# Dealing six projection units of the short convolution out between the attention heads of an encoder block

## The chip, the cores and the metric

One core of a Trainium2 chip runs the whole block. The metric is the device time of one execution in microseconds; lower is better. The engines are TensorE (PE: matmuls, and its weight loads as PEld), VectorE (DVE), ScalarE (ACT), GpSimd (POOL) and SyncE (SP), whose queue starts the weight transfers.

## What is computed

One residual block on 512 tokens of 1024 values, all in float32: a SwiGLU feed-forward half step (1024 to 2816 and back), the mixer, a second such half step, and a last RMS norm. Each part begins with an RMS norm whose scale and shift come from a vector c. The mixer, in which the change lies:

```python
z = h @ w_in[l]                                   # 1024 -> 2240 columns
xb, xc, xu, cq, ckv, kr = jnp.split(z, cuts, axis=-1)
y_a = short_conv_mixer(xb, xc, xu, conv_w[l])     # xb * causal 3-tap conv(xc * xu), 512 wide
y_b = mla(cq, ckv, kr, positions, ...)            # 4 heads, keys of 128 + 64 rotary, values of 128
y_a = group_rmsnorm(y_a, g[:512], 8)              # 8 groups of 64
y_b = group_rmsnorm(y_b, g[512:], 4)              # one norm for each head
x = x + g2 * (jnp.concatenate([y_a, y_b], axis=-1) @ w_out[l])
```

In `mla` queries are `rmsnorm(cq) @ w_uq`, keys and values `rmsnorm(ckv) @ w_ukv`; attention is block-causal over chunks of 64 tokens, with a softmax in float32.

## The kernel before, in words

**Units.** Activations lie transposed: 128 features on the partitions, 512 tokens along the row. Weights come in units of up to 128 x 1024 values (512 KB). For each unit SP loads `raw`, ACT copies it rounded into `wh` (`split_hi`, L408), DVE or POOL subtracts to get the rest `wl` (`split_lo`, L1118; POOL's `unit_lo`, L381), and PE multiplies. Each tile of 128 inputs costs three matmuls (high by high, high by low, low by high: `three`, L722), so a unit of eight tiles has 24 matmuls of 512 columns. `raw`, `wh` and `wl` have two buffers each, taken by the parity of the unit's number: the load of unit n waits for the split of n-2 (`lo_ready`), ACT's copy for the product of n-2 (`unit_done`).

**Order.** Every engine has its instructions written out in program order, and runs them in that order; counting semaphores tie them together. Units are numbered: `U_Z` (six units for ckv, cq and the rotary key), `U_CONV` (three for each of the four convolution tiles: C, U, B), `U_V` (two for the values), `U_H` (one for each head: query, query rotary, key), `U_O` (eight half units of the output product), then the second feed-forward. Convolution units run back to back in a loop before `U_V`. For tile i, ACT copies C out of PSUM, DVE multiplies it by U, sums three taps (`cacc`, L1391 and L1394) and multiplies by B into `yc` (L1398).

**Attention.** `head_part(h, 0..2)` makes the query, its rotary part and the key; ACT copies each rounded (`qnh`, `qrh`, `knh`: L570, L574, L576), DVE multiplies the rotary part by cosines (L1434) and subtracts the rests (L1426, L1439, L1441). `scores(h, q)` for four query tiles, longest first; `maximum` on DVE (L1474), `exp` on ACT (L584), `divide` on DVE once the four are done (L1483, L1488), `turn(h, q)` on PE (transposes, L970), `turned_hi` on ACT (L591), `turned_lo` on DVE (L1493), `head_product(h)`. PE interleaves scores(h+1, q) with turn(h, q); parts of heads 2 and 3 stand between.

**Norms.** A norm is a column sum on PE (`norm_sum`, L741) into PSUM bank 7 (`norm_bank`), `root` on ACT (L422), `inverse` on DVE (L1134 to L1146: reciprocal, rounding, rest, two diagonals), `norm_spread` on PE (L748), and `apply` on DVE (L1166), whose result ACT rounds (L432) and DVE subtracts (L1157). The convolution's group norm has `conv_square` (ACT, L536), `conv_sum` (PE, L922, into bank 4), `conv_root` (ACT, L628), `conv_inverse` and `conv_split` (DVE, L1462 to L1469), `conv_spread` (PE, L930 and L931), `apply_conv` (DVE, L1451), `conv_hi` (ACT, L432) and `conv_lo` (POOL, L388). In before the group norm comes first and head 0's norm after it. ACT loads a table when it goes from exponentials to square roots or back (ACT_TABLE_LOAD). `warm` (L755) are nine matmuls with no use but to keep PE at work; one call stands after the value units.

Of the kernel before, what the change touches and what calls it, by code (L numbers as in the profile page):

```python
# [90 lines left out]
FREE = 1  # L91


def hybrid_block(nc, x, c, positions, ada_w, ada_b, norm_ffn1_g, ffn1_w1, ffn1_w3, ffn1_w2, norm_mix_g,
                 w_in, conv_w, q_norm_g, w_uq, kv_norm_g, w_ukv, out_norm_g, w_out, norm_ffn2_g,
                 ffn2_w1, ffn2_w3, ffn2_w2, final_norm_g, consts, out):
    with ExitStack() as ctx:  # L97
# [304 lines left out]
        def _(act):  # L402
# [118 lines left out]
            with act.Fori(0, CT // 2) as m:  # L521
                for s in range(6):
                    p, which = divmod(s, 3)
                    if which == 0:

                        act.wait_ge(unit_done, U_CONV + 6 * m + s + 1)
                        act.wait_ge(u_conv, FREE + 2 * m + p)
                        act.activation(cbuf[:, :], pb[CONV_BANKS[p][0]][:, :], ACT.Copy).then_inc(c_copied, 1)
                    split_hi(U_CONV + 6 * m + s + 2, s % 2, 48 * m + landed(U_CONV + s + 2))
# [1101 lines left out]
```

## Time and profile before

| | us |
|---|---|
| median of 3 runs | 1052.82 |
| lowest, highest | 1052.28, 1054.54 |
| span of the profiled execution | 1052.8 |
| PE busy | 1009.5 (96%) |
| PE weight loads busy | 831.4 (79%) |
| DVE busy | 564.9 (54%) |
| ACT busy | 400.6 (38%) |
| POOL busy | 66.3 (6%) |
| mean granted clock of PE | 0.974 |

The profile gives no time of the profiled execution other than its span, which is the median of the runs to 0.02 us; nothing lies around it to be added. Busy shares are of the whole span, so they say which engine is near its limit, but a stage has to be looked at by itself: by stretches of time (with the clock granted to PE, 1.00 for 2.4 GHz and 0.50 for 1.2), by the waits of PE, and by the instructions in order of time. In such rows "[1.23 <-DVE ubuf]" means that the engine was idle for 1.23 us just before, until that instruction of DVE was done. A matmul of 512 columns is shown with 0.39 us but the next starts 0.23 behind it.

### The profile page before, as it was taken

The page shows a single profiled execution, that of the slowest core. Times are in us where ns is not written, and L with a number is a line of the kernel's source. Part 1 is how long each engine was busy: PE and PEld are TensorE (multiplying, and loading weights), DVE is VectorE, ACT ScalarE, POOL GpSimd, SP SyncE. Part 2 cuts the span into 40 slices and gives each one's busy share as a digit, 9 for nine tenths or more (in the row PEclk, how much of TensorE's full clock was granted, in tenths as well). Part 3 has the DMA queues.
Part 4 walks back from the last instruction along what each step waited for, and adds up shares of the span by engine and source line. Part 5 has one row for each costly group of instructions (what it writes and reads, how often), then busy time and mean ns, then how long its engine had stood idle before and what let it go on. Part 6 is the DMA issues. An engine that isn't in the chain of part 4 may idle for free. (4 is left out here: it accounts for less than half of the span.)

```text
span 1052.8 us, 13254 instructions
## 1 busy us (share of the span) xinstructions
PE 1009.5 (96%) x4505; PEld 831.4 (79%) x4505; DVE 564.9 (54%) x754; ACT 400.6 (38%) x568; POOL 66.3 (6%) x79
## 2 busy tenths in 40 slices
PE   3699999999999999999999989999999999999997
PEld 3678888888888888888867777788888888888886
DVE  5868777787753333754377645744434333333332
ACT  3254434444332222442255443353444444332222
POOL 2411111011000000000000310000000000000000
PEclk9599999999999999999999799999999999999999
DMA  9547766687633324123221101223323333333232
GB/s 333 175 133 249 242 198 211 206 256 235 202 92 93 92 90 115 50 81 100 80 65 40 41 23 58 80 80 100 98 85 96 99 100 100 94 93 93 90 109 81
DMA packets 176622, 127.82 MB, mean 121 GB/s; under 512 B 5069, under 2 KB 165718, under 8 KB 176598
## 3 DMA queue, kind: packets, MB, share of 16 engines
q1 hardware_dynamic: 168534, 98.14, 31.1%
q0 software_dynamic: 8064, 29.36, 8.4%
q8 instruction: 14, 0.23, 0.1%
q14 instruction: 10, 0.08, 0.0%
HBM read 125.39 MB, written 2.10 MB: 121 GB/s over the span
## 5 line engine op out<-in xcount | busy, mean ns | idle before, releaser
L722 PE MATMUL pb<-hh,wh 128*128 128x512 f32 x912 | 358.5, 393 | 5.0 <-DVE hl L1159 2.8
L722 PE MATMUL pb<-hh,wl 128*128 128x512 f32 x912 | 355.8, 390 | 0.0
L722 PE MATMUL pb<-hl,wh 128*128 128x512 f32 x912 | 355.7, 390 | 0.0
L1118 DVE TENSOR_TENSOR wl<-raw,wh 128x1024 fp32r<-128x1024 f32 x156 | 191.1, 1225 | 275.1 <-ACT wh L408 275.0
L408 ACT ACTIVATE wh<-raw 128x1024 fp32r<-128x1024 f32 x163 | 172.5, 1059 | 410.5 <-PE pb L722 410.5
L722 PEld LDWEIGHTS pb<-hh,wh 128*128 128x128 f32 x912 | 171.5, 188 | 46.5 <-DVE hl L1159 7.2
L722 PEld LDWEIGHTS pb<-hh,wl 128*128 128x128 f32 x912 | 171.6, 188 | 36.2
L722 PEld LDWEIGHTS pb<-hl,wh 128*128 128x128 f32 x912 | 171.7, 188 | 34.5
L722 PE MATMUL pb<-gh,wh 128*128 128x512 f32 x352 | 137.0, 389 | 0.0
L722 PE MATMUL pb<-gh,wl 128*128 128x512 f32 x352 | 136.9, 389 | 0.0
L722 PE MATMUL pb<-gl,wh 128*128 128x512 f32 x352 | 136.9, 389 | 0.0
L722 PEld LDWEIGHTS pb<-gl,wh 128*128 128x128 f32 x352 | 66.1, 188 | 13.8
L722 PEld LDWEIGHTS pb<-gh,wl 128*128 128x128 f32 x352 | 66.1, 188 | 13.7
L722 PEld LDWEIGHTS pb<-gh,wh 128*128 128x128 f32 x352 | 66.1, 188 | 13.7
L1193 DVE SCALAR_TENSOR_TENSOR acc<-ada_ring,silu_c,acc 128x1024 f32<-128x1024 f32 x49 | 62.8, 1282 | 1.0
L1237 DVE TENSOR_TENSOR gbuf<-sbuf,pb 128x512 f32<-128x512 f32 x44 | 30.2, 686 | 58.4 <-PE pb L722 58.3
L445 ACT ACT_TABLE_LOAD x44 | 56.5, 1283 | 0.8
L417 ACT ACTIVATE sq<-xres 128x512 f32<-128x512 f32 (+1 forms) x32 | 20.2, 631 | 90.2 <-DVE xres L1247 85.2
L373 POOL DMA_DIRECT2D ada_ring<-in_ada_w_dram x56 | 29.8, 532 | 211.3 <-DVE acc L1191 112.8
L1247 DVE SCALAR_TENSOR_TENSOR xres<-pb,half_gates,xres 128x512 f32 (+1 forms) x16 | 12.0, 751 | 46.3 <-PE pb L722 46.3
L452 ACT ACTIVATE gh<-gbuf 128x512 f32 x44 | 27.9, 634 | 10.7 <-DVE gbuf L1237 10.7
L1240 DVE TENSOR_TENSOR gl<-gbuf,gh 128x512 f32 (+1 forms) x44 | 30.1, 683 | 0.0
(193 smaller groups left out, 763.2 us busy)
## 6 DMA issues: line engine op xcount, KB each, us to landing
raw<-in_ffn_w_dram SPq DMA_DIRECT2D x104, 512.0 KB, 3.8
ada_ring<-in_ada_w_dram POOLq DMA_DIRECT2D x56, 512.0 KB, 5.1
raw<-in_ffn_w_dram SPq DMA_DIRECT2D x32, 448.0 KB, 3.4
raw<-in_w_in_dram SPq DMA_DIRECT2D x17, 512.0 KB, 3.9
ada_start<-in_ada_w_dram SPq DMA_DIRECT2D x8, 1024.0 KB, 16.4
raw<-in_w_out_dram SPq DMA_DIRECT2D x8, 512.0 KB, 3.4
x_nat<-in_x_dram SPq DMA_DIRECT2D x1, 2048.0 KB, 10.5
out_dram<-o_nat SPq DMA_DIRECT2D x8, 256.0 KB, 2.9
```

The lines of the kernel that those rows point to most:

```text
L373: pool.dma_start(ada_ring[:, k % 4, :], adav[:, k, bass.ds(j * D_MODEL + 2 * D_MODEL, D_MODEL)]) \
L408: act.activation(wh[par][:, :], raw[par][:, :], ACT.Copy).then_inc(hi_ready, 1)
L417: act.activation(sq[:, slot, :], src, ACT.Square).then_inc(sq_ready, 1)
L445: act.activation(vcol[:, V_COLS + 9:V_COLS + 10], kst[:, K_COLS:K_COLS + 1], ACT.Sigmoid)
L452: act.activation(gh[:, bass.ds(i, 1), :], gbuf[:, :].unsqueeze(1), ACT.Copy).then_inc(gh_ready, 1)
L722: last = pe.matmul(o, a, b, start=start and j == 0 and t == 0, stop=stop and j == len(pairs) - 1 and t == 2)
L1118: dve.tensor_tensor(wl[par][:, :], raw[par][:, :], wh[par][:, :].bitcast(F32), ALU.subtract).then_inc(lo_ready, 1)
L1193: dve.scalar_tensor_tensor(out=acc[:, :], in0=src, scalar=silu_c[:, k:k + 1], in1=acc[:, :], op0=ALU.mult, op1=ALU.add).then_inc(ada_step, 1)
L1237: dve.tensor_tensor(gbuf[:, :], sbuf[:, :], pb[1][:, :], ALU.mult).then_inc(g_ready, 1)
L1240: dve.tensor_tensor(gl[:, bass.ds(i, 1), :], gbuf[:, :].unsqueeze(1), gh[:, bass.ds(i, 1), :].bitcast(F32), ALU.subtract).then_inc(gl_read ...
L1247: dve.scalar_tensor_tensor(out=xd, in0=pb[bank][:, :].unsqueeze(1), scalar=gate, in1=xd, op0=ALU.mult, op1=ALU.add).then_inc(x_upd, 1)
```

## The change

The six units of convolution tiles 2 and 3 (c20 to c22, c30 to c32) leave the loop ahead of the value units and stand between the steps of the heads: c20 before head 0's parts, c21 before head 1's, quarters of c22 behind the score steps of head 0, quarters of c30 behind those of head 1, quarters of c31 behind the transposes of head 0, c32 after head 0's product. Parts of heads 2 and 3 move behind c32. All four orders and SP's loads are rewritten to match; `head_parts_hi`, `head_parts_lo` and the helpers that interleaved scores and transposes become single steps. The key now goes through bank 0. Head 0's norm comes before the group norm, whose column sums now go to `norm_bank` (so `conv_sum(0)` waits for the instruction that applies head 0's norm), and its spreads stand before and inside the first output unit. The nine warm matmuls after the value units are gone. In the diff below the two long orders of ACT and DVE are given as they are after the change, without the lines removed.

```diff
-U_V = U_CONV + 3 * CT
-U_H = U_V + KT
-U_O = U_H + HEADS
+U_V = U_CONV + 3 * (CT // 2)
+LATE = ("c20", "h0", "c21", "h1", "c22", "c30", "c31", "c32", "h2", "h3")
+U_LATE = {name: U_V + KT + j for j, name in enumerate(LATE)}
+U_H = tuple(U_LATE[f"h{h}"] for h in range(HEADS))
+U_O = U_V + KT + len(LATE)
 U_A2 = U_O + DT
...
-AP_BASE = {N_FFN1: 0, N_MIX: 8, N_KV: 16, N_Q: 18, N_HEAD: 25, N_FFN2: 29, N_FINAL: 37}
-AP_CONV = 21
-SPREAD = {N_FFN1: 0, N_MIX: 1, N_KV: 2, N_Q: 3, N_HEAD: 8, N_HEAD + 1: 9, N_HEAD + 2: 10, N_HEAD + 3: 11, N_FFN2: 12}
-SPREAD_CONV = 4
+AP_BASE = {N_FFN1: 0, N_MIX: 8, N_KV: 16, N_Q: 18, N_HEAD: 21, N_HEAD + 1: 26, N_HEAD + 2: 27, N_HEAD + 3: 28,
+   N_FFN2: 29, N_FINAL: 37}
+AP_CONV = 22
+AP_OUT = tuple(AP_CONV + j for j in range(CT)) + tuple(AP_BASE[N_HEAD + h] for h in range(HEADS))
+SPREAD = {N_FFN1: 0, N_MIX: 1, N_KV: 2, N_Q: 3, N_HEAD: 4, N_HEAD + 1: 9, N_HEAD + 2: 10, N_HEAD + 3: 11, N_FFN2: 12}
+SPREAD_CONV = 5
...
-CONV_BANKS = ((0, 1, 2), (3, 4, 6))
+CONV_BANKS = ((0, 1, 2), (3, 4, 6), (6, 2, 6), (2, 1, 2))
...
+    conv_load(U_LATE["c20"], 2, 0)
+    head_load(0)
+    conv_load(U_LATE["c21"], 2, 1)
+    head_load(1)
+    conv_load(U_LATE["c22"], 2, 2)
+    conv_load(U_LATE["c30"], 3, 0)
+    conv_load(U_LATE["c31"], 3, 1)
+    conv_load(U_LATE["c32"], 3, 2)
+    head_load(2)
+    head_load(3)
...
+    unit_lo(U_O)
     conv_lo(0)
-    unit_lo(U_O)
+    unit_lo(U_O + 1)
     conv_lo(1)
     conv_lo(2)
-    unit_lo(U_O + 1)
     conv_lo(3)
...
+    def conv_copy(i):
+        act.wait_ge(unit_done, U_LATE[f"c{i}0"] + 1)
+        if i == 2:
+            act.wait_ge(u_ready, AP_BASE[N_Q] + QT)
+        else:
+            act.wait_ge(conv_step, FREE + 3 * i)
+        act.activation(cbuf_late[:, :], pb[CONV_BANKS[i][0]][:, :], ACT.Copy).then_inc(c_copied, 1)
...
+    for t in range(QT):
+        norm_hi(AP_BASE[N_Q] + t, cqh[:, t, :])
+    act.wait_ge(kr_dup, 1)
+    act.activation(krh[:, :], pb[5][:, :], ACT.Copy).then_inc(krh_ready, 1)
+    unit_hi(U_LATE["c20"])
     for t in range(TT):
         act.wait_ge(unit_done, U_V + KT)
         act.activation(vh[:, t, :], pb[t][:, :], ACT.Copy).then_inc(vh_ready, 1)
+    head_hi(0)
+    conv_copy(2)
+    unit_hi(U_LATE["c21"])
+    nope_hi(0)
+    rope_hi(0)
+    key_hi(0)
     head_hi(1)
+    unit_hi(U_LATE["c22"])
+    nope_hi(1)
+    rope_hi(1)
+    key_hi(1)
+    unit_hi(U_LATE["c30"])
+    for q in range(TT):
+        exp(0, q)
+    unit_hi(U_LATE["c31"])
+    for q in range(TT):
+        exp(1, q)
+    conv_copy(3)
+    turned_hi(0, 0)
+    unit_hi(U_LATE["c32"])
+    turned_hi(0, 1)
+    turned_hi(0, 2)
+    turned_hi(0, 3)
+    conv_square(0)
+    conv_square(1)
     head_hi(2)
     head_out(0)
     head_square(0)
+    head_hi(3)
+    nope_hi(2)
+    rope_hi(2)
+    root(N_HEAD, V_HEAD)
+    key_hi(2)
+    unit_hi(U_O)
+    head_norm_hi(0)
+    exp(2, 0)
+    turned_hi(1, 0)
+    nope_hi(3)
+    exp(2, 1)
+    conv_square(2)
+    turned_hi(1, 1)
+    rope_hi(3)
+    exp(2, 2)
+    conv_square(3)
+    turned_hi(1, 2)
+    key_hi(3)
+    exp(2, 3)
+    turned_hi(1, 3)
+    conv_root()
     unit_hi(U_O + 1)
     head_out(1)
+    head_square(1)
+    for q in range(TT):
+        turned_hi(2, q)
+        exp(3, q)
+    conv_hi(0)
+    conv_hi(1)
+    head_out(2)
+    conv_hi(2)
     conv_hi(3)
     unit_hi(U_O + 2)
+    turned_hi(3, 0)
+    turned_hi(3, 1)
     root(N_HEAD + 1, V_HEAD)
...
+            three(pb[0][:, :], [(cols(wh[b], k), cols(wl[b], k), cqh[:, k, :], cql[:, k, :])
+                                for k in range(QT)], True, True).then_inc(q_done, 1)
         elif part == 1:
-            pe.wait_ge(q_roped, h)
+            if h == 0:
+                pe.wait_ge(vl_ready, 2)
+            else:
+                pe.wait_ge(q_roped, h)
+            if h == 2:
+                pe.wait_ge(u_conv, FREE + CT)
...
-            pe.wait_ge(pl_ready, 3 * (h - 1) + part + 1)
-        if part < 2:
-            three(pb[part][:, :], [(cols(wh[b], QT * part + k), cols(wl[b], QT * part + k), cqh[:, k, :], cql[:, k, :])
-                                   for k in range(QT)], True, True).then_inc(q_done, 1)
-        else:
-            three(pb[2][:, :], [(cols(wh[b], 2 * QT + k), cols(wl[b], 2 * QT + k), ckh[:, k, :], ckl[:, k, :])
+            pe.wait_ge(pl_ready, 3 * h + 1)
+            three(pb[0][:, :], [(cols(wh[b], 2 * QT + k), cols(wl[b], 2 * QT + k), ckh[:, k, :], ckl[:, k, :])
...
+    def late_bank_free(i, which):
+        if i == 2 and which == 1:
+            pe.wait_ge(vl_ready, 3)
+        if (i, which) in ((2, 2), (3, 2)):
+            pe.wait_ge(c_copied, i + 1)
+        if i == 3 and which == 0:
+            pe.wait_ge(u_conv, FREE + 3)
+        if i == 3 and which == 1:
+            pe.wait_ge(q_roped, 2)
+    def conv_quarter(i, which, quarter):
+        n = U_LATE[f"c{i}{which}"]
+        b = n % 2
+        if quarter == 0:
+            unit(n)
+            late_bank_free(i, which)
+        ks = range(2 * quarter, 2 * quarter + 2)
+        last = three(pb[CONV_BANKS[i][which]][:, :], [(cols(wh[b], k), cols(wl[b], k), hh[:, k, :], hl[:, k, :]) for k in ks],
+                     quarter == 0, quarter == 3)
+        if quarter == 3:
+            last.then_inc(unit_done, 1)
+    def conv_unit(i, which):
+        for quarter in range(4):
+            conv_quarter(i, which, quarter)
...
     def conv_sum(j):
         pe.wait_ge(csq_ready, j + 1)
         if j == 0:
-            pe.wait_ge(u_conv, FREE + CT)
-        pe.matmul(pb[4][SQUARE * j:SQUARE * (j + 1), :], kst[:, K_HALF:K_HALF + SQUARE], sq[:, j % 2, :],
+            pe.wait_ge(u_ready, AP_BASE[N_HEAD] + 1)
+        pe.matmul(norm_bank[SQUARE * j:SQUARE * (j + 1), :], kst[:, K_HALF:K_HALF + SQUARE], sq[:, j % 2, :],
                   start=True, stop=True).then_inc(group_summed, 1)
...
+        if h == 0 and q == 1:
+            pe.wait_ge(yc_ready, FREE + 3)
...
-    conv_sum(0)
-    conv_sum(1)
     v_unit(0)
     v_unit(1)
-    warm(WARM_HEADS)
-    head_part(0, 0)
+    conv_unit(2, 0)
+    head_unit(0)
+    conv_unit(2, 1)
+    head_unit(1)
+    for q in range(TT):
+        scores(0, q)
+        conv_quarter(2, 2, q)
+    for q in range(TT):
+        scores(1, q)
+        conv_quarter(3, 0, q)
+    for q in range(TT):
+        turn(0, q)
+        conv_quarter(3, 1, q)
+    head_product(0)
+    conv_unit(3, 2)
+    head_part(2, 0)
+    head_sum(0)
+    head_part(2, 1)
+    norm_spread(N_HEAD)
+    head_part(2, 2)
+    conv_sum(0)
+    scores(2, 0)
+    turn(1, 0)
+    head_part(3, 0)
+    conv_sum(1)
+    scores(2, 1)
+    turn(1, 1)
+    head_part(3, 1)
     conv_sum(2)
-    head_part(0, 1)
+    scores(2, 2)
+    turn(1, 2)
+    head_part(3, 2)
     conv_sum(3)
-    head_part(0, 2)
-    head_unit(1)
-    scores(0, 0)
-    for q in range(1, TT):
-        scores(0, q)
-        head_part(2, q - 1)
-    scores_and_turns(0)
-    head_product(0)
-    head_unit(3)
-    scores_and_turns(1, {0: lambda: conv_spread(0), 2: lambda: conv_spread(1), 3: lambda: conv_spread(2)})
+    scores(2, 3)
+    turn(1, 3)
     head_product(1)
+    for q in range(TT):
+        scores(3, q)
+        turn(2, q)
+    conv_spread(0)
+    head_product(2)
+    conv_spread(1)
+    out_begin(0)
+    out_steps(0, (0,))
+    conv_spread(2)
+    out_steps(0, (1,))
     conv_spread(3)
-    head_sum(0)
-    scores_and_turns(2)
-    norm_spread(N_HEAD)
-    head_product(2)
-    out_unit(0)
-    head_sum(1)
+    out_steps(0, (2, 3)).then_inc(unit_done, 1)
     turn(3, 0)
     turn(3, 1)
+    head_sum(1)
     out_begin(1)
     out_steps(1, (0, 1))
     turn(3, 2)
     turn(3, 3)
+    norm_spread(N_HEAD + 1)
     out_steps(1, (2, 3)).then_inc(unit_done, 1)
     head_product(3)
-    norm_spread(N_HEAD + 1)
     out_begin(2)
+    head_sum(2)
     out_steps(2, (0, 1))
-    head_sum(2)
+    norm_spread(N_HEAD + 2)
     out_steps(2, (2, 3)).then_inc(unit_done, 1)
-    norm_spread(N_HEAD + 2)
...
+    dve.wait_ge(krh_ready, 1)
+    dve.tensor_tensor(krl[:, :], pb[5][:, :], krh[:, :].bitcast(F32), ALU.subtract).then_inc(krl_ready, 1)
+    unit_lo(U_LATE["c20"])
     for t in range(TT):
         dve.wait_ge(vh_ready, t + 1)
         dve.tensor_tensor(vl[:, t, :], pb[t][:, :], vh[:, t, :].bitcast(F32), ALU.subtract).then_inc(vl_ready, 1)
+    head_lo(0)
+    unit_lo(U_LATE["c21"])
+    nope_lo(0)
+    turn_rope(0)
+    rope_lo(0)
+    key_lo(0)
     head_lo(1)
+    conv_u(2, U_LATE["c21"], cbuf_late, cbuf_late)
+    unit_lo(U_LATE["c22"])
+    nope_lo(1)
+    conv_taps(2, cbuf_late, yc[:, 2, :])
+    turn_rope(1)
+    rope_lo(1)
+    key_lo(1)
+    unit_lo(U_LATE["c30"])
+    for q in range(TT):
+        maximum(0, q)
+    conv_y(2, U_LATE["c22"], yc[:, 2, :])
+    maximum(1, 0)
+    unit_lo(U_LATE["c31"])
+    maximum(1, 1)
+    divide(0)
+    maximum(1, 2)
+    maximum(1, 3)
+    turned_lo(0, 0)
+    unit_lo(U_LATE["c32"])
+    turned_lo(0, 1)
+    turned_lo(0, 2)
+    turned_lo(0, 3)
+    conv_u(3, U_LATE["c31"], cbuf_late, cbuf_late)
+    conv_taps(3, cbuf_late, yc[:, 3, :])
+    divide(1)
+    head_lo(2)
+    conv_y(3, U_LATE["c32"], yc[:, 3, :])
+    head_lo(3)
+    nope_lo(2)
+    turn_rope(2)
+    rope_lo(2)
+    inverse(N_HEAD)
+    key_lo(2)
+    apply_head(0)
+    maximum(2, 0)
+    turned_lo(1, 0)
+    nope_lo(3)
+    maximum(2, 1)
+    turned_lo(1, 1)
+    turn_rope(3)
+    rope_lo(3)
+    maximum(2, 2)
+    turned_lo(1, 2)
+    key_lo(3)
+    maximum(2, 3)
+    turned_lo(1, 3)
+    divide(2)
     conv_inverse(0)
+    maximum(3, 0)
+    conv_inverse(1)
+    turned_lo(2, 0)
+    maximum(3, 1)
     conv_inverse(2)
+    turned_lo(2, 1)
+    maximum(3, 2)
     conv_inverse(3)
+    turned_lo(2, 2)
+    maximum(3, 3)
     conv_split()
+    turned_lo(2, 3)
+    apply_conv(0)
+    divide(3)
+    apply_conv(1)
+    apply_conv(2)
     apply_conv(3)
+    turned_lo(3, 0)
+    turned_lo(3, 1)
     inverse(N_HEAD + 1)
+    turned_lo(3, 2)
+    turned_lo(3, 3)
     apply_head(1)
     inverse(N_HEAD + 2)
     apply_head(2)
```

## Rows read from the trace of the kernel before

**Rows 1.** The page, busy time of each engine.

```profile
PE 1009.5 (96%) x4505; PEld 831.4 (79%) x4505; DVE 564.9 (54%) x754; ACT 400.6 (38%) x568; POOL 66.3 (6%) x79
```

**Rows 2.** Windows of the core: length, busy times, PEclk, DMA share, GB/s.

```profile
531.30:618.30 87.00, 83.38 (x362) 63.10 (x361) 59.58 (x130) 46.11 (x106) 9.83 (x6) 0.90 0.13 40
...
573.80:577.20 3.40, 3.40 (x13) 3.16 (x14) 2.26 (x4) 2.05 (x4) 0.00 (x0) 0.56 0.00 0
591.30:604.90 13.60, 12.35 (x37) 9.40 (x38) 8.94 (x16) 6.13 (x12) 7.21 (x5) 0.50 0.23 78
632.20:635.60 3.40, 3.40 (x11) 2.75 (x10) 0.69 (x1) 0.99 (x2) 0.00 (x0) 0.50 0.24 83
```

**Rows 3.** Waits of PE from 498 to 670 us: total, times, longest.

```profile
PE pb L748 <- DVE diag L1146: 2.4, 2, 2.3
PE pb L741 <- DVE ubuf L1451: 1.2, 1, 1.2
PE pb L722 <- DVE wl L1118: 1.2, 1, 1.2
PE pb L722 <- DVE ptl L1493: 1.1, 2, 0.8
PE pb L722 <- ACT probs L584: 0.8, 1, 0.8
PE pb L922 <- ACT sq L536: 0.4, 1, 0.4
```

**Rows 4.** PE in order of time: the first conv sums, the warm matmuls.

```profile
533.10 1.56 PE L922 MATMUL pb<-sq,kst 128*32 128x512 f32 x4 [0.36 <-ACT sq L536]
...
540.21 1.75 PE L755 MATMUL pb<-exact 128*128 128x384 f32 x9
```

**Rows 5.** ACT in order of time: start, length, instruction, idle before.

```profile
515.15 1.06 ACT L408 ACTIVATE wh<-raw 128x1024 fp32r<-128x1024 f32 x1 [4.38 <-PE pb L722]
...
531.47 1.06 ACT L408 ACTIVATE wh<-raw 128x1024 fp32r<-128x1024 f32 x1 [4.38 <-PE pb L722]
...
536.53 0.63 ACT L432 ACTIVATE cqh<-ubuf 128x512 fp32r<-128x512 f32 x1 [0.76 <-DVE ubuf L1166]
...
599.09 1.28 ACT L422 ACT_TABLE_LOAD   x1
600.39 0.26 ACT L422 ACTIVATE rms<-pb,kst 128x4 f32<-128x4 f32 x1
...
606.50 0.69 ACT L584 ACTIVATE probs<-pb,nmax_s 128x512 f32<-128x512 f32 x1
```

**Rows 6.** DVE in order of time.

```profile
532.56 1.23 DVE L1118 TENSOR_TENSOR wl<-raw,wh 128x1024 fp32r<-128x1024 f32 x1 [0.23 <-ACT wh L408]
...
550.66 0.69 DVE L1441 TENSOR_TENSOR knl<-pb,knh 128x512 fp32r<-128x512 f32 x1 [0.29 <-ACT knh L576]
...
578.84 0.94 DVE L1462 RECIPROCAL sq<-sq 128x128 f32<-128x128 f32 x1
...
593.25 4.44 DVE L1488 TENSOR_SCALAR probs<-probs,rinv 128x512 f32<-128x512 f32 x4
...
600.68 0.18 DVE L1134 RECIPROCAL rrms<-rms 128x4 f32<-128x4 f32 x1 [2.33 <-ACT rms L422]
...
601.79 0.68 DVE L1146 TENSOR_TENSOR diag<-kst,rrms_l 128x512 fp32r<-128x512 f32 x1
...
611.06 1.27 DVE L1488 TENSOR_SCALAR probs<-probs,rinv 128x512 f32<-128x512 f32 x4
...
631.29 0.75 DVE L1166 SCALAR_TENSOR_TENSOR ubuf<-o_raw,vcol,pb 128x512 f32<-128x512 f32 x1 [0.64 <-issue]
```

**Rows 7.** The page, transfers of w_in: KB each, us to landing.

```profile
raw<-in_w_in_dram SPq DMA_DIRECT2D x17, 512.0 KB, 3.9
```

**Rows 8.** POOL in order of time.

```profile
593.87 1.38 POOL L388 TENSOR_TENSOR hl<-ubuf,hh 128x512 fp32r<-128x512 f32 x1 [0.37 <-ACT hh L432]
595.21 2.40 POOL L381 TENSOR_TENSOR wl<-raw,wh 128x1024 fp32r<-128x1024 f32 x1
```

More of the change, by code:

```diff
@@ L189, in hybrid_block @@
         assert e3 <= 229344, e3
+        (cbuf_late,), _ = place(region + 2 * KT * SEQ * 4, ("cbuf_late", [P, SEQ], F32))
         (xg,), _ = place(hh_at, ("xg", [P, DT, SEQ], F32))
@@ L519, in _, with unit_hi @@
             root(N_Q, Q_LORA)
[L521 to L529, printed above, removed]
+            for s in range(6):
+                i, which = divmod(s, 3)
+                if which == 0:
+                    act.wait_ge(unit_done, U_CONV + s + 1)
+                    act.wait_ge(u_conv, FREE + i)
+                    act.activation(cbuf[:, :], pb[CONV_BANKS[i][0]][:, :], ACT.Copy).then_inc(c_copied, 1)
+                split_hi(U_CONV + s + 2, s % 2, landed(U_CONV + s + 2))
+            def unit_hi(n):
+                split_hi(n, n % 2, landed(n))
+            def conv_copy(i):
[5 more added lines that the diff above has]
+                act.activation(cbuf_late[:, :], pb[CONV_BANKS[i][0]][:, :], ACT.Copy).then_inc(c_copied, 1)
             def conv_square(j):
@@ L548, in head_hi @@
             def head_hi(h):
-                b = h % 2
-                n = U_H + h
+                n = U_H[h]
+                b = n % 2
+                before = sum(U_H[g] % 2 == b for g in range(h))
                 act.wait_ge(raw_landed[b], landed(n))
-                act.wait_ge(kn_landed[b], 16 * (h // 2 + 1))
+                act.wait_ge(kn_landed[b], 16 * (before + 1))
                 act.wait_ge(unit_done, n - 1)
@@ L593, in turned_hi @@
                                ACT.Copy).then_inc(pth_ready, 1)
-            def exps_and_turned(h, behind=None):
-                for q in range(TT):
-                    turned_hi(h, q)
-                    exp(h + 1, q)
-                    if behind is not None and q in behind:
-                        behind[q]()
             def head_out(h):
@@ L981, in head_product @@
                 last.then_inc(pv_done, 1)
-            def scores_and_turns(h, behind=None):
-                for q in range(TT):
-                    scores(h + 1, q)
-                    turn(h, q)
-                    if behind is not None and q in behind:
-                        behind[q]()
             def head_sum(h):
                 pe.wait_ge(gsq_ready, h + 1)
-                norm_sum(N_HEAD + h, gsq, AP_BASE[N_HEAD] + h)
+                norm_sum(N_HEAD + h, gsq, AP_BASE[N_HEAD + h])
             def out_begin(o):
@@ new lines, in conv_y @@
+            def conv_y(i, n, sums):
+                dve.wait_ge(conv_step, FREE + 3 * i + 3)
+                dve.wait_ge(unit_done, n + 1)
+                dve.tensor_tensor(yc[:, i, :], sums[:, :], pb[CONV_BANKS[i][2]][:, :], ALU.mult).then_inc(yc_ready, 1)
+            for s in range(6):
+                i, which = divmod(s, 3)
+                if which == 1:
+                    conv_u(i, U_CONV + s, cbuf, ubufc)
+                if which == 2:
+                    conv_taps(i, ubufc, cacc)
+                    conv_y(i, U_CONV + s, cacc)
+                split_lo(U_CONV + s + 2, s % 2)
@@ L1532, in _ @@
-            maxima_and_turned(1, {0: lambda: apply_conv(0), 2: lambda: apply_conv(1), 3: lambda: apply_conv(2)}, first=1)
-            divide(2)
-            apply_conv(3)
-            inverse(N_HEAD)
-            maxima_and_turned(2)
-            divide(3)
-            apply_head(0)
-            for q in range(TT):
-                turned_lo(3, q)
+            turned_lo(2, 3)
[3 more added lines that the diff above has]
+            apply_conv(2)
+            apply_conv(3)
```

195 lines of the change are left out of this document (68 added, 127 removed).

## The prediction

> **What bounds the kernel now.** I read the page's busy times first: TensorE (PE) is busy 96% of the span [rows 1], so a new order of the same matmuls can only pay by filling PE's idle time or by getting back a slow clock. Next the granted clock by stretch: in the 87 us between the last convolution unit and the end of the first output unit PE runs at 1.2 GHz instead of 2.4 for 3.4 us and again for 13.6 us, and once more for 3.4 us behind that [rows 2]. Then the PE waits from the projection to the end of the output product: 7.1 us in six groups [rows 3]. Last the order of ScalarE (ACT), VectorE (DVE) and GpSimd (POOL) in that stretch, because the diff rewrites all four queues. The profiled execution spans 1052.8 us, the median of the runs is 1052.82, so sum and median are taken against the same time. 0.2% (2.1 us) is about what a measurement of this kernel can tell from no change.
>
> **What PE executes.** The same matmuls in another order, less the nine warm matmuls, which last 1.7 us [rows 4]. One unit of 24 matmuls takes 5.44 us (three units lie between the ACT splits at 515.15 and 531.47 [rows 5]), a quarter unit 1.36. So the sum is: waits and slow clock taken away, against waits and slow clock made. I follow the new queues in the time of before, up to the end of the first output unit (618.3), where both orders have done the same work.
>
> **Gone, at most.** Warm 1.7. The waits of before up to 618.3: 7.1 less the 2.4 and the 1.2 behind it, 3.5 [rows 3]. The slow clock: (3.4 + 13.6 − 1.2 idle) / 2 = 7.9 [rows 2, 3]. Together 13.1.
>
> **Made, one by one.** PE runs in program order, so each wait below holds everything behind it.
> 1. The first late unit (c20). The value units now end at 538.3: they lose the two conv sums ahead of them, which began at 533.1 behind a wait of 0.4 and took 1.5 [rows 4], and start 1.9 earlier. ACT writes the last query tile until 537.16, then krh (0.5 more), then the unit's split (1.06); DVE's half takes 1.23 [rows 5, 6]: ready at 540.0. Wait 1.7, just what the warm matmuls filled.
> 2. Heads 0 and 1: each step of scores or transposes has a dense quarter behind it. DVE's new work there (six splits of 1.23, the product, the taps) fits: 0.3 us for scores(0,2), whose exponential stands behind the split of c30; otherwise nothing, and ACT and DVE have one to three us of slack at each step. The SP queue issues the same loads, only reordered; each waits for the split two units before, some 5 us before its turn, and lands in 3.9 [rows 5, 7]. Cost 0. If that cover is gone, a late load costs at most its 3.9 once.
> 3. **norm_spread of head 0.** This is the large one. It stands between parts 1 and 2 of head 2, and needs root(N_HEAD), which on ACT stands behind rope_hi(2), which needs the DVE product on part 1. So from the issue of part 1's last matmul: 0.2 until it is drained, 0.69 product, 0.63 copy, 1.28 table load (square root after exponentials), 0.26 root, 1.79 inverse and diagonals (600.68 to 602.47) [rows 5, 6] = 4.85; the spread's first half can issue before the second diagonal is there, which gives 0.15 back. Wait 4.7.
> 4. **conv_sum(0)** now writes norm_bank, so it waits for apply_head(0), which on DVE stands behind key_lo(2), that is behind part 2, the matmuls just ahead: 0.2 + 0.6 + 0.69 + 0.75 = 2.25 [rows 5, 6].
> 5. conv_sum(3): its square stands on ACT behind exp(2,2), which hangs by a chain of nine short steps (about 5.0 us, copies and subtractions of 0.4 to 0.7) against 3.8 of PE work: 1.15. Then head_product(1), behind exp(2,3) and the last transpose's two copies: 1.7.
> 6. scores(3,2) behind the table load and exp(3,0): 1.28 + 0.69 + 0.2 after the transposes' copy [rows 5], against one step of PE work: 1.2 (0.8 in before [rows 3]).
> 7. conv_spread(0): four reciprocals of 0.94 and the split (about 1.1) now lie among the maxima of head 3 instead of in idle time: they end 2.15 after the last transpose [rows 6].
> 8. The first output unit. Before, its inputs were ready long ahead. Now apply_conv, ACT's copy and POOL's subtraction (1.3 to 1.4) run just ahead of the matmuls, and divide(3) stands between apply_conv(0) and (1) while POOL makes a unit split of 2.4. The row of before for just that pair is 4.44 us for the four scalings where 1.27 is normal, ending with POOL's instruction (597.69 and 597.61) [rows 6, 8]. I take 4.4: waits of 0.4, 2.0, 1.35 and 1.6 = 5.35. With 1.27 it would be 2.2.
>
> Sum of new waits: 1.7 + 0.3 + 4.7 + 2.25 + 2.85 + 1.2 + 2.15 + 5.35 = 20.5.
>
> One rule speaks to points 3 and 6. Rows: the table load takes 1.28 and the root begins 0.02 behind it [rows 5]. The Trainium skill, ScalarE: Activation LUTs, What ACT_TABLE_LOAD costs, adds a drain of about 1.38 us to each switch. By that page point 3 would be about 6.1, an estimate; the rows show no such gap, and the sum stays with 1.28.
>
> **The clock, made.** Before, a wait of 2.4 with short matmuls around it was followed by 3.4 us at half clock, and one of 0.8 amid scores and transposes likewise [rows 2, 3]. A fall costs (3.4)/2 = 1.7. I expect one fall after points 3 and 4, one after 5 and 6, one in 7 and 8: 5.1. Bounds: none, 0; or half clock throughout from point 5 on, as in the 13.6 us of before, when PE's about 22 us of work there cost up to 10 more, less what the waits absorb.
>
> **Behind the first output unit.** norm_spread(N_HEAD+1) now stands earlier, and ACT's root ahead of the last transposes; POOL's split no longer falls on the diagonals (the 2.4 of before). Its wait becomes 1.1, the next spread's 0.6: −0.7; the 3.4 us of slow clock behind it go: −1.7. Together −2.4. The 1.2 behind DVE's split of an output unit stays. From there on nothing differs.
>
> **Sum.** −13.1 + 20.5 + 5.1 − 2.4 = +10.1: 1052.8 + 10.0, rounded = **1062.8 us**. The heads 0 and 1 do what interleaving should do, but head 0's norm chain in series costs more than it wins.
>
> **Rivals.**
> A. *Density wins* (faster). The dense quarters keep the clock at 2.4 GHz all through, and ACT and DVE run far enough ahead that only points 1, 3 and 4 are left: −13.1 − 2.4 + 1.7 + 7.0 = −6.8: 1046. For it: the 17 us of slow clock lie where scores and transposes stand alone [rows 2]. Against: head 3's scores and head 2's transposes still stand alone, and points 7 and 8 are chains through three engines. It decides if all waits but those of points 1, 3 and 4, and the clock's cost, stay below 6.8 us together. The Trainium skill, TensorE: Matmul & The Clock Gate, says that the default clock is the throttled one and activity releases it, which favours this rival; the trace agrees only in part: in the 13.6 us at half clock PE was busy for 12.35 [rows 2]. Chance 0.12.
> B. *Waits real, clock full, the chain at the output unit short* (divide(3) gets through before POOL locks it out). −13.1 + 20.5 − 3.15 − 1.0 − 2.4 = +0.85, where the 3.15 are point 8's 5.35 less 2.2, and the 1.0 is absorbed in points 5 to 7: 1053.7. Chance 0.10, half of it within 0.2%.
> C. *The clock stays down* from point 3 to the output unit: +10 where the forecast has +5.1, and a fall of 1.7 in the tail: 1069. For it: 12 us of waits in the last 20 us before that point. Chance 0.13.
> The forecast (one to three falls, and a few us either way in the waits, 1056 to 1067): 0.65.
>
> **Range.** From between B and the forecast's foot to C: 1053 to 1071; outside it A and a little above C, under 0.2. Faster 0.13 (A and a bit of B), same 0.06, slower 0.81.
>
> **What the profile would show.** Right: PE's wait for the diagonals of head 0 near 4.7 us between parts 1 and 2 of head 2, 2.2 for conv_sum(0), waits for POOL's hl in the first output unit, no wait over 0.5 in heads 0 and 1, full clock there, two more table loads. Wrong: PE waits in that stretch below 13 us together, or slow clock over 15 us from head 2 on, or DVE or ACT late already in head 1 (splits of the late units as the wait), which would make it slower in a place I hold free.

## The result, and the profile after

The changed kernel takes 1063.91 us (median of 4, 1062.52 to 1064.40) against 1053.09 (median of 4, 1052.28 to 1054.54): ratio 1.0103, 95% interval 1.0090 to 1.0116. It is slower by 10.8 us. The profiled execution spans 1062.1 us, and its own time is 1063.8: 1.7 us lie around the span, as in every later run that gives both. So the span of before, 1052.8, belongs to an execution of about 1054.5, one of its longest, and not to the median as the prediction had it. Comparing the two profiles gives 9.3 us of loss instead of 10.8. The same kernel's executions differ by 3 to 4 us, which has to be kept in mind for every difference below 2 us. In some of the variants below the longer executions have the lower mean clock; in the kernel before the two do not go together (about 1051.3 at 0.976, 1052.8 at 0.980, 1054.5 at 0.977).

The page of the changed kernel, busy times:

```profile
PE 1009.0 (95%) x4496; PEld 827.0 (78%) x4496; DVE 565.4 (53%) x754; ACT 403.9 (38%) x570; POOL 66.4 (6%) x79
```

PE is busy as long as before [rows 1] in a longer span, without its nine warm matmuls. ACT has two instructions more, the two table loads. The waits of PE from 498 to 670 us (total, times, longest):

```profile
PE pb L807 <- DVE diag L1255: 4.2, 1, 4.2
PE pb L781 <- DVE wl L1227: 3.0, 2, 1.8
PE pb L1014 <- DVE ubuf L1275: 2.2, 1, 2.2
PE pb L1022 <- DVE group_rl L1584: 1.8, 1, 1.8
PE pb L781 <- DVE ptl L1608: 1.4, 1, 1.4
PE pb L781 <- POOL hl L410: 1.3, 1, 1.3
PE pb L781 <- ACT probs L620: 1.0, 1, 1.0
PE pb L1014 <- ACT sq L570: 0.2, 1, 0.2
PE pb L781 <- POOL wl L403: 0.2, 1, 0.2
```

This answers to [rows 3]. The two large ones at the diagonals and at `ubuf` are head 0's norm; `wl` holds the first late unit (1.8) and the unit of 1.2 that was there before; the rest stand one each at head_product(1), scores(3,2), conv_spread(0), the first output unit and conv_sum(3). Windows of the changed kernel: from the new first late unit to c32's end, the heads 2 and 3 up to conv_spread(0), then up to the end of the first output unit, the tail, and three stretches at half clock:

```profile
498.60:565.50 66.90, 65.08 (x300) 52.51 (x300) 41.16 (x81) 30.15 (x63) 0.00 (x0) 1.00 0.25 68
565.50:612.40 46.90, 36.10 (x156) 24.64 (x154) 25.92 (x56) 23.43 (x48) 2.36 (x1) 0.93 0.10 34
612.40:630.70 18.30, 17.03 (x45) 11.16 (x46) 7.49 (x10) 3.01 (x5) 7.52 (x5) 0.63 0.10 30
630.70:648.50 17.80, 17.46 (x91) 14.30 (x90) 8.99 (x17) 7.51 (x13) 4.78 (x2) 1.00 0.18 59
574.60:578.00 3.40, 3.07 (x7) 2.27 (x8) 0.88 (x2) 0.00 (x0) 0.00 (x0) 0.54 0.00 0
581.50:584.90 3.40, 3.40 (x8) 2.09 (x7) 1.72 (x1) 1.13 (x1) 1.17 (x1) 0.52 0.32 91
612.60:626.30 13.70, 13.70 (x33) 8.73 (x33) 6.64 (x8) 2.38 (x4) 6.25 (x4) 0.51 0.13 39
```

In heads 0 and 1 the clock is 1.00 and PE is idle only once. Then come 46.9 us with 36.1 of work. The first output unit ends at 630.7 instead of 618.3 (12.4 later), and in the tail about 3.1 us come back: the 2.4 at the diagonals is a wait no more, nor is there a stretch at half clock [rows 2, 3].

Head 0's norm chain in the changed kernel, ACT and DVE in order of time (start, length):

```profile
571.45 0.63 ACT L608 ACTIVATE qrh<-rope 128x512 fp32r<-128x512 f32 x1 [3.06 <-DVE rope L1547]
572.10 1.28 ACT L444 ACT_TABLE_LOAD   x1
573.39 0.27 ACT L444 ACTIVATE rms<-pb,kst 128x4 f32<-128x4 f32 x1
```

```profile
570.72 0.69 DVE L1547 TENSOR_TENSOR rope<-pb,cs 128x512 f32<-128x512 f32 x1 [1.38 <-PE pb L781]
...
573.69 0.18 DVE L1243 RECIPROCAL rrms<-rms 128x4 f32<-128x4 f32 x1 [0.89 <-ACT rms L444]
...
579.32 0.69 DVE L1556 TENSOR_TENSOR knl<-pb,knh 128x512 fp32r<-128x512 f32 x1 [3.85 <-ACT knh L612]
579.93 0.74 DVE L1275 SCALAR_TENSOR_TENSOR ubuf<-o_raw,vcol,pb 128x512 f32<-128x512 f32 x1
```

Rotary product, copy, table load, root, inverse, each begins when the one before it ends. conv_sum(0) then starts at 580.81, right behind the last row.

### The profile page after: what moved, and what is told of

It is laid out like the page before. It is cut to its first block, busy times and chain, and to the rows that moved or that the text cites. A ratio compares the mean times of both kernels' runs of the same rounds, so it can differ in the third digit from the quotient of the medians.

```text
span 1062.1 us, 13114 instructions
## 1 busy us (share of the span) xinstructions
PE 1009.0 (95%) x4496; PEld 827.0 (78%) x4496; DVE 565.4 (53%) x754; ACT 403.9 (38%) x570; POOL 66.4 (6%) x79
## 4 chain that ended last, share of the span: by engine, by line
PE 86%; DVE 3%; ACT 2%; issue 2%; POOL 0%; POOLq 0%; DVEq 0%; ACTq 0%
PE pb L781 83%; DVE ubuf L1275 1%; PE pb L814 1%; DVE hl L1268 1%; ACT wh L430 0%; PE pb L800 0%; PE pb L807 0%; PE pb L1041 0%; PE pb L1014 0%; DVE wl L1227 0%; POOL hl L410 0%; ACT L444 0%; POOLq L103 0%; PE pb L1207 0%; POOL wl L403 0%
## 5 line engine op out<-in xcount | busy, mean ns | idle before, releaser
L781 PEld LDWEIGHTS pb<-gh,wh 128*128 128x128 f32 x352 | 66.1, 188 | 13.9
L781 PEld LDWEIGHTS pb<-gh,wl 128*128 128x128 f32 x352 | 66.1, 188 | 13.7
L781 PEld LDWEIGHTS pb<-gl,wh 128*128 128x128 f32 x352 | 66.1, 188 | 13.6
L403 POOL TENSOR_TENSOR wl<-raw,wh 128x1024 fp32r<-128x1024 f32 x5 | 11.9, 2384 | 312.6 <-ACT wh L430 312.6
```

What stands on the lines that cost most here:

```text
L403: pool.tensor_tensor(wl[n % 2][:, :], raw[n % 2][:, :], wh[n % 2][:, :].bitcast(F32), ALU.subtract).then_inc(lo_ready, 1)
L781: last = pe.matmul(o, a, b, start=start and j == 0 and t == 0, stop=stop and j == len(pairs) - 1 and t == 2)
```

## The experiments

Twelve kernels ran, all of them told here, each against the kernel before. "Changed" is the changed kernel. Times are medians, in us.

**1. The norm chain out of series (e1_chain).** On the changed kernel:

```diff
 # PE
-head_part(2, 1); norm_spread(N_HEAD); head_part(2, 2); conv_sum(0); scores(2, 0); turn(1, 0)
+head_part(2, 1); head_part(2, 2); norm_spread(N_HEAD); turn(1, 0); scores(2, 0); conv_sum(0)
 # ACT
-nope_hi(2); rope_hi(2); root(N_HEAD, V_HEAD); key_hi(2)
+nope_hi(2); root(N_HEAD, V_HEAD); rope_hi(2); key_hi(2)
 # DVE
-nope_lo(2); turn_rope(2); rope_lo(2); inverse(N_HEAD); key_lo(2)
+nope_lo(2); inverse(N_HEAD); turn_rope(2); rope_lo(2); key_lo(2)
```

> Head 0's norm chain taken out of series: ACT's root(N_HEAD) stands before rope_hi(2), DVE's inverse before the rotary product of head 2, and PE makes part 2 of head 2, then norm_spread, turn(1, 0) and scores(2, 0) before conv_sum(0). Theory (the waits of 4.2 and 2.2 us for this chain, and the two falls of the clock behind them, are a large part of the loss): the two waits shrink to about 2 together and one fall at least goes, 1063.9 - 4.4 - 1.7 to 3.4 = 1056 to 1058. Rival (the work behind is held by ACT and DVE anyway, so PE only arrives earlier at later waits): 1062 to 1064, with the 6.4 us found again in the waits at conv_sum(3), head_product(1) and conv_spread(0).

Measured 1054.37 (10 runs, 1052.57 at a mean clock of 0.981 to 1057.82 at 0.971), ratio to before 1.0014 (1.0002 to 1.0027). Waits of PE, the largest:

```profile
PE pb L781 <- DVE wl L1227: 3.0, 2, 1.8
PE pb L781 <- DVE knl L1556: 1.5, 1, 1.5
PE pb L781 <- DVE ptl L1608: 1.4, 1, 1.4
```

The 6.4 us have become 1.5, at scores(2,0), and 9.5 us are won, more than the waits and two falls of the clock. The rival, that the time would be found again further on, falls.

**2. The old order of the norms, the units still dealt out (v2_oldnorm).** The group norm first, head 0's norm behind it:

```diff
-AP_BASE: N_HEAD: 21; AP_CONV = 22; SPREAD: N_HEAD: 4; SPREAD_CONV = 5
+AP_BASE: N_HEAD: 25; AP_CONV = 21; SPREAD: N_HEAD: 8; SPREAD_CONV = 4
 # PE
-head_part(2, 0); head_sum(0); head_part(2, 1); norm_spread(N_HEAD); head_part(2, 2)
+head_unit(2)
...
 out_steps(0, (2, 3)).then_inc(unit_done, 1)
+head_sum(0)
...
 out_steps(1, (0, 1))
+norm_spread(N_HEAD)
 # ACT and DVE: root, inverse and apply of the heads moved back to match
```

> The dealing out of the six units kept, the order of the norms as in the kernel before: group norm first, head 0's norm behind it (its sum after the first output unit, its spread inside the second, the other heads' norms moved back to match). Theory (of the two parts of the change the order of the norms is the one that costs): the waits of 4.2 and 2.2 us and the falls behind them go, and about 1 to 2 us of new waits come in the tail: 1063.9 - 6.4 - 3.4 + 2 = 1056. Rival (the dealing out itself costs, by the squeezed group norm between the heads and the output unit): 1060 or more.

Measured 1055.09 (10 runs, 1052.15 to 1056.75), ratio 1.0022 (1.0010 to 1.0034). So of the 10.8 us the way the norms stand costs 8.8, and the dealing out, as it is done here, 2.0 to 2.4 (in this series the kernel before took 1052.68). It is not the order as such: e1_chain keeps head 0's norm first and takes no longer. The remaining waits of v2_oldnorm include 1.8 at the group's rest, 1.4 at head_product(1) and 1.8 at the first late unit, as in the changed kernel.

**3. What the clock costs (w1_fill, w2_fill, w3_fill).** Warm matmuls put into the waits; no order moves:

```diff
 head_part(2, 1)
+warm(22)                    # w1, w3
 norm_spread(N_HEAD)
 head_part(2, 2)
+warm(11)                    # w1, w3
 conv_sum(0)
...
+warm(7, 2)                  # w3, ahead of head_product(1)
...
+warm(5, 2)                  # w2, w3, ahead of scores(3, 2)
...
+warm(9, 2)                  # w2, w3
 conv_spread(0)
```

> Warm matmuls put into two waits of the changed kernel: 22 before norm_spread of head 0 (wait 4.2 us) and 11 before conv_sum(0) (wait 2.2 us). No order is changed and no wait gets shorter, so this measures the clock alone. Theory (idle time behind these waits brings the clock down for two stretches of 3.4 us): both falls go, 2 to 3.4 us faster, 1060.5 to 1062. Rival (the clock falls for another reason, as the short matmuls of the scores): 1064.

> Warm matmuls put into the wait for exp(3, 0) (5) and the wait before conv_spread(0) (9) of the changed kernel. Theory (the 13.6 us at half clock from conv_spread(0) on follow from idle time before it): the stretch goes or is one of 3.4 us, and since the units behind then wait for POOL and DVE a little more, 3 to 6 us faster: 1058 to 1061. Rival (it follows from scores and transposes, which keep PE busy with short matmuls, as before the change): 1064, with the same stretch at 0.50.

> The changed kernel with all its larger waits between head 2 and the output unit filled with warm matmuls: 22 before norm_spread of head 0, 11 before conv_sum(0), 7 before head_product(1), 5 before scores(3, 2), 9 before conv_spread(0). No order changes. Theory (the clock is a third of the loss): the granted clock is 1.00 all through and 4 to 6 us are won against the changed kernel, 1058 to 1060. Rival (only the falls behind head 0's norm cost, those further on are covered by the chain through DVE, ACT and POOL): 1060 to 1061, as with two fills.

w1_fill: 1060.66 (1059.82 to 1061.36), 3.3 below the changed kernel. In its profile both falls behind head 0's norm are gone, and conv_sum(3) starts 26.7 instead of 29.4 us behind head_sum(0): they were worth 2.7. What else it won came later, where it has 3.4 and 6.8 us at half clock instead of 13.7. w3_fill: 1060.07 (1059.76 to 1061.57), 3.8 below; in its profiled execution, one of the long ones (1061.52), 3.4 us at half clock lie at 508 and 6.8 in the first output unit, so the clock was not full all through as expected.

w2_fill: 1063.97, but its four executions are two at 1061.5 and 1062.5 with a mean clock of 0.981 and 0.978, and two at 1065.5 and 1065.7 with 0.972, so the median tells nothing. Its profile (1062.47) does: no half clock from conv_spread(0) to the first output unit's end, and that stage lasts 15.4 us where the changed kernel has 18.3. The stage and PE's waits in it:

```profile
613.90:629.30 15.40, 11.14 (x44) 7.36 (x45) 7.54 (x10) 3.01 (x5) 7.53 (x5) 1.00 0.10 36
PE pb L781 <- POOL hl L410: 2.7, 3, 1.3
PE pb L1022 <- DVE ubuf L1569: 1.5, 1, 1.5
```

So the 13.7 us at half clock cost 2.9 there, not the 6.8 that half their length would be: PE's idle time in the stage is 4.3 without them and 1.3 with them. One execution of each shows this.

**4. The lock (x_div, w4_fill_div).** In both divide(3) goes behind the four apply_conv; w4_fill_div has the fills of w3_fill besides.

```diff
 apply_conv(0)
-divide(3)
 apply_conv(1)
 apply_conv(2)
 apply_conv(3)
+divide(3)
```

> The changed kernel with one step moved on DVE: divide(3) behind apply_conv(3) instead of between apply_conv(0) and apply_conv(1). In the changed kernel these four scalings last 4.4 us (1.3 alone), ending with POOL's unit split, while apply_conv(1) waits behind them. Theory (the first output unit is bound by the chain spread, apply, round, subtract, of which this lock is the longest link, and not by the slow clock, since filling the waits ahead took the slow clock away and won nothing): apply_conv(1) comes 3 to 4 us earlier and 1.5 to 3 us are won: 1061 to 1062.5. Rival (the slow clock sets that stage): 1064, since PE's work at half clock covers the chain.

> As w3_fill, and divide(3) behind apply_conv(3). With the clock kept up, the price of the lock stands alone. Theory (the chain at the first output unit counts once the clock does not cover it): apply_conv(1) comes some 4 us earlier, the waits there fall from about 4.5 to about 2.5, and 2 us are won against w3_fill. Rival (the next links, POOL's subtraction behind each spread, are as late): same as w3_fill.

x_div: 1064.28 (1062.36 to 1066.24), no gain in the median. w4_fill_div: 1058.32 (1056.54 to 1058.55) against w3_fill's 1059.76 to 1061.57: 1.8 us, as the theory said, and the ranges do not touch. DVE in w3_fill, and then in w4_fill_div:

```profile
612.85 4.42 DVE L1609 TENSOR_SCALAR probs<-probs,rinv 128x512 f32<-128x512 f32 x4
617.19 0.73 DVE L1572 SCALAR_TENSOR_TENSOR ubuf<-yc,vcol,pb 128x512 f32<-128x512 f32 x1
```

```profile
613.34 0.75 DVE L1572 SCALAR_TENSOR_TENSOR ubuf<-yc,vcol,pb 128x512 f32<-128x512 f32 x1 [1.98 <-PE pb L1023]
```

Counted from conv_spread(0) (611.2 and 609.8), the second apply_conv comes at 6.0 and at 3.5. The stage up to the first output unit's end takes 17.2 and 13.9 us:

```profile
611.20:628.40 17.20, 14.19 (x45) 9.13 (x46) 7.56 (x10) 3.01 (x5) 7.54 (x5) 0.80 0.09 31
```

```profile
609.80:623.70 13.90, 11.12 (x44) 7.37 (x45) 5.55 (x10) 3.01 (x5) 7.45 (x5) 1.00 0.12 39
```

Part of this difference is clock (0.80 against 1.00), which is why the medians differ by less. The same stage in five profiles:

| | divide(3) | us at half clock | PE idle | length |
|---|---|---|---|---|
| changed | ahead | 13.7 | 1.3 | 18.3 |
| w3_fill | ahead | 6.8 | 3.0 | 17.2 |
| w2_fill | ahead | none | 4.3 | 15.4 |
| x_div | behind | 3.4 | 1.9 | 14.5 |
| w4_fill_div | behind | none | 2.8 | 13.9 |

At full clock divide(3) in its old place costs 1.5 us (15.4 against 13.9), the slow clock alone 2.9 (18.3 against 15.4). The theory of x_div holds in this stage. It does not show in the median: x_div's profiled execution has 10.2 us at half clock behind head 0's norm where the changed kernel has 6.8, and 3.4 more on the way, and comes to conv_spread(0) at 614.6 instead of 612.4.

**5. The first late unit (x_c20).** ACT's and DVE's halves of c20's split moved ahead of the last query tile's copy and of krh and krl:

```diff
-for t in range(QT): norm_hi(...); krh; unit_hi(c20)   # ACT
+for t in range(QT): norm_hi(...), behind t == 1: unit_hi(c20); krh
-krl; unit_lo(c20)                                     # DVE
+unit_lo(c20); krl
```

> The changed kernel with the split of the first late unit ahead of the last query tile's copy and of the rotary key on ACT, and ahead of the rotary key's rest on DVE. Theory (PE's wait of 1.8 us for this unit is ACT's and DVE's order): the wait falls to about 0.8 to 1.0 and 0.8 to 1.0 us are won, 1063. Rival (the value units or the transfer hold it): no change of the wait.

The wait falls from 1.8 to 1.0, as expected; DVE still has the query tiles' rests ahead of the split. 1062.68 (1060.80 to 1063.19), 1.2 below the changed kernel, of which 0.8 is the wait; the rest is within the scatter.

**6. The warm matmuls (b_nowarm).** The kernel before without `warm(WARM_HEADS)`.

> The kernel before without its nine warm matmuls behind the value units. Theory of the prediction's sum (the 1.7 us of warm matmuls are PE time that can be had back only where nothing else is awaited): part 0 of head 0 waits for its split, ready 0.5 us behind the value units, so 1.1 us are won, 1051.9. Rival (the wait behind the warm matmuls brings the clock down or the vl subtractions hold the parts): 1053 or more.

1052.74 (1051.35 to 1054.80), ratio 0.9999 (0.9990 to 1.0008): nothing. The theory falls. Behind the value units PE now waits for the value rests:

```profile
541.83 0.47 PE L722 MATMUL pb<-cqh,wh 128*128 128x512 f32 x1 [1.50 <-DVE vl L1511]
```

The part starts at 541.83; in before, behind the warm matmuls, at 541.88. From there on both kernels have the same orders, so their profiles also show what half clock is worth. The 3.4 us at half clock from 573.8 on are missing here, and everything behind comes 1.6 us earlier. The 13.6 us of before are 6.8 here, and that brings only 0.2 more, for PE's wait at head 0's column sum is 3.4 instead of 1.2:

```profile
PE pb L741 <- DVE ubuf L1450: 3.4, 1, 3.4
```

**7. A version that beats both (c1_early, c2_early, c3_early).** From v2_oldnorm with x_c20's edit; the group norm pulled forward:

```diff
 # PE, c1
-head_unit(2); conv_sum(0); scores(2, 0); turn(1, 0); head_part(3, 0); conv_sum(1); scores(2, 1) ...
+head_part(2, 0); conv_sum(0); head_part(2, 1); conv_sum(1); head_part(2, 2); turn(1, 0); conv_sum(2)
+scores(2, 0); conv_sum(3); head_part(3, 0); scores(2, 1) ...
-for q: scores(3, q); turn(2, q)
+for q: scores(3, q); turn(2, q); conv_spread(q)
 # PE, c1: the first output unit runs without spreads between its steps
 # ACT, c1: conv_square(2), (3) and conv_root() to ahead of exp(2, 0); conv_hi among the steps of head 3
 # DVE: conv_inverse(0..3) among the steps of head 2, conv_split() ahead of maximum(3, 0), divide(3) behind apply_conv(3)
 # PE, c2
-head_product(1); scores(3, 0)
+scores(3, 0); head_product(1)
 # PE, c2: norm_spread(N_HEAD) from behind out_steps(1, (0, 1)) to behind turn(3, 3)
 # ACT, c2: turned_hi(1, 1) behind rope_hi(3); exp(3, 0) ahead of unit_hi(U_O + 1)
 # DVE, c2
-maximum(2, 1); conv_inverse(2); turned_lo(1, 1); turn_rope(3); rope_lo(3); maximum(2, 2); conv_inverse(3)
+maximum(2, 1); turn_rope(3); rope_lo(3); turned_lo(1, 1); maximum(2, 2); conv_inverse(2)
 # PE, c3
-for q: ...; turn(2, q); conv_spread(q); then head_product(2)
+for q: ...; turn(2, q); conv_spread(q - 1); then head_product(2); conv_spread(3)
 # DVE, c3
-inverse(N_HEAD); turned_lo(3, 0); turned_lo(3, 1)
+turned_lo(3, 0); turned_lo(3, 1); inverse(N_HEAD)
 # DVE, c3: apply_conv(0..2) one score step later
 # ACT, c3
-root(N_HEAD); head_square(1); turned_hi(3, 0); turned_hi(3, 1)
+turned_hi(3, 0); turned_hi(3, 1); root(N_HEAD); head_square(1)
```

> The dealing out kept, the norms in the order of before, and the group norm pulled forward: its sums stand between the parts of head 2, its root ahead of exp(2, 0), its reciprocals among the steps of head 2 and its spreads behind the four score steps of head 3, so that the first output unit finds its inputs ready; the first late unit's split ahead of the rotary key; divide(3) behind the spreads. Theory (what the dealing out wins by a full clock in heads 0 and 1 was eaten by the norms that it pushed together): waits at the group's rest (1.8) and in the first output unit (1.2) and 0.8 at the first late unit go against v2_oldnorm, 1055.1 - 3 to 4 = 1051 to 1052, below the kernel before by 1 to 2 us. Rival (the two more table loads and the denser DVE queue in head 2 make new waits of the same size): 1054 to 1056.

> c1_early with its one large wait (3.9 us at head_product(1)) attacked: head 3's rotary product goes ahead of the transposes' copies on DVE and ACT, two of the group's reciprocals move behind, and scores(3, 0) stands ahead of head_product(1). Theory (that wait is the DVE order): it falls below 1, one fall of the clock goes with it, 1050.5 - 3 to 4 = 1047. Rival (DVE is simply full there, 3.9 us of reciprocals more than before): 1049.5 to 1051, the wait found again before conv_spread(0).

> c2_early with its two new waits attacked: each group spread stands one score step later and the last behind head_product(2), so that the group's rest (wait of 1.9 us) is ready; and head 0's inverse goes behind the first two transposes' rests on DVE, so that these, which read PSUM, no longer stand behind scalings that POOL's unit split holds up (wait of 2.2 us at turn(3, 2)). Theory: both waits fall below 0.5 and the time to 1047, 0.5% below the kernel before. Rival (the waits only move, to the first output unit, whose last input now comes later, and to the spread of head 0): 1049 to 1050.

c1_early: 1050.47, ratio 0.9972 (0.9961 to 0.9982). The waits at the group's rest and in the first output unit are gone, a new one of 3.9 stands at head_product(1). c2_early: 1049.69, with 12 executions from 1046.30 to 1054.96, ratio 0.9974 (0.9959 to 0.9989); its 3.9 is gone, but 1.4 now stands at scores(3, 0), and 1.9 and 2.2 at the group's rest and at turn(3, 2). Against c1_early this is no gain that can be told, as the rival said. c3_early: **1045.40** (5 runs, 1045.02 to 1046.27), ratio 0.9929 (0.9915 to 0.9942). Its waits of PE above 0.3 us:

```profile
PE pb L782 <- DVE wl L1229: 2.2, 2, 1.2
PE pb L782 <- DVE knl L1558: 1.4, 1, 1.4
PE pb L808 <- DVE diag L1257: 1.0, 1, 1.0
PE pb L782 <- DVE hl L1270: 0.9, 3, 0.4
```

The 1.9 and the 2.2 are gone. The 2.2 was for the most part a matter of order and not of POOL: in c2_early DVE stood idle until head 0's root was there (613.65), which on ACT came ahead of the transposes' copies, then made the inverse, and only then the rests that PE waited for. POOL held up one step in this by 0.5 us. c3_early is 7.5 us faster than the kernel before and 18.5 faster than the changed one, so with the norms rearranged the units can be dealt out at a gain. No run has the rearranged norms without the dealing out, so how much of the 7.5 each brings is not shown.

## Why the prediction was right

1062.8 was forecast with a range of 1053 to 1071, and 1063.91 was measured. Of the signs named, those of being right came: the waits for head 0's diagonals and for conv_sum(0), a wait for POOL's `hl`, no wait over 0.5 and full clock in heads 0 and 1, two more table loads. But one sign of being wrong came too: 20.5 us at half clock from head 2 on, where over 15 was to count against it, and the waits (13.9) are just above the 13 that was to do so. By its time this is the forecast's case, by its clock rival C's. The sum was right to 1 us (+10.1 against +10.8 by the medians and +9.3 by the two profiles), but its terms were not: two errors of 5 to 7 us cancelled. That was partly luck and partly one and the same effect, as the clock took the place of waits.

- **Waits.** Forecast 20.5, measured 13.9 up to the first output unit's end (the table above without the 1.2 and the 0.2 behind it). Point by point: the first late unit 1.7 and 1.8; heads 0 and 1 0.3 and none; norm_spread of head 0 4.7 and 4.2; conv_sum(0) 2.25 and 2.2; conv_sum(3) 1.15 and 0.2; head_product(1) 1.7 and 1.4; scores(3,2) 1.2 and 1.0; conv_spread(0) 2.15 and 1.8. All eight are within 1 us. The term that was mis-sized is **point 8**, 5.35 against 1.3. Its mechanism is there: divide(3) takes 4.40 us in the changed kernel, ending with POOL, as in the row of before [rows 6, 8]:

```profile
614.47 4.40 DVE L1603 TENSOR_SCALAR probs<-probs,rinv 128x512 f32<-128x512 f32 x4
618.79 0.73 DVE L1566 SCALAR_TENSOR_TENSOR ubuf<-yc,vcol,pb 128x512 f32<-128x512 f32 x1
```

```profile
615.09 1.33 POOL L410 TENSOR_TENSOR hl<-ubuf,hh 128x512 fp32r<-128x512 f32 x1 [32.42 <-ACT hh L454]
616.39 2.40 POOL L403 TENSOR_TENSOR wl<-raw,wh 128x1024 fp32r<-128x1024 f32 x1
```

But PE was at half clock just there, so that its matmuls took the time that I had put down as waits. With the clock up (w2_fill) the waits of that unit are 1.5 for DVE and 2.7 for POOL, 4.2 against the 5.35 of the forecast. Moving divide(3) away is then worth 1.5 in the profiles and 1.8 in the medians (experiment 4). The Trainium skill (SBUF — State Buffer, Who interferes with whom) has a lock between POOL and DVE in its two-port modes: whichever issues first holds a shared pair of ports for the whole instruction, and the other blocks. The trace agrees in that DVE's scalings end with POOL's instruction, at 618.87 and 618.79.

- **The clock, made.** Forecast 5.1 for three falls of 3.4; measured 3.4, 3.4 and 13.7 us at half clock up to 626.3, which is (20.5 − 0.3 idle) / 2 = 10.1. I had this as the upper bound and called it rival C. That two falls follow the waits of head 0's norm is shown: w1_fill fills them and has neither; they were worth 2.7. That the 13.7 are worth their 6.8 is refuted: w2_fill's profile has none of them and is 2.9 shorter there, with 3.0 more of idle time. So the three stretches cost 5.6 together, near the 5.1, and the waits at full clock would be about 16.9. Adding waits and slow clock as if they were independent was the error in both terms.

- **Not in the sum.** Each of the twelve quarters behind a score step or a transpose takes 1.49 instead of 1.36 us, 1.6 in all: behind a score step or transposes the first matmul is followed 0.31 to 0.34 us later, the others 0.23. In a unit behind a unit all are 0.23 apart, so it is not the new group as such. A score step of head 0 ends and a quarter begins:

```profile
531.02 0.50 PE L781 MATMUL pb<-hh,wh 128*128 128x512 f32 x1
531.36 0.40 PE L781 MATMUL pb<-hl,wh 128*128 128x512 f32 x1
531.59 0.39 PE L781 MATMUL pb<-hh,wl 128*128 128x512 f32 x1
```

- **Gone.** 13.1 was the profile's own: 1.7 + 3.5 + 7.9. But in the kernel before the warm matmuls cost nothing: without them PE waits 1.5 for the value rests (experiment 6). And the slow clock of before was put in at its full half, though there too 6.8 us less of it brought only 0.2 (experiment 6). As an account of the two profiles, each with its waits and its slow clock, it does close: −13.1 + 13.9 + 10.1 + 1.6 = 12.5, and the first output unit ends 12.4 later.

- **The tail.** Forecast −2.4, measured −3.1; the wait at the second norm_spread is none (1.1 was forecast), the third's also none.

- **Table loads.** Forecast at 1.28 without a drain; in the changed kernel the load begins 0.02 us behind the end of the copy and the root 0.01 behind the load's end. The Trainium skill (ScalarE: Activation LUTs, What ACT_TABLE_LOAD costs) adds a drain of about 1.38 to each switch; the trace does not show it, and point 3 came out at 4.2, not at 6.1.

- **Rival A** fell where it was expected to: the clock is 1.00 in heads 0 and 1, as it said, but the chains are there.

Open: the 2.9 and the 2.7 us for the slow clock rest on one profile of each kernel, and the executions scatter by as much. And e1_chain won 9.5 us in the medians where its waits (4.9) and two falls (2.7) make 7.6; the last 1.9 lie within its scatter of 5 us, and the two profiles differ by 6.8. Nor does idle time alone account for every fall: the 13.6 us at half clock of before begin at 591.3, amid scores and transposes, when PE had been busy for 11.16 of the last 11.30 us.
